# Two transformer blocks in one kernel: the modulation product moved from TensorE to VectorE, and the weight stream put into five shared slots

## The reference

```python
def first_block(x, ...):
    h = rmsnorm(x); dq, dk, dv, sq, sk, sv = split(h @ w_qkv)
    diff_o = rmsnorm(diff_attention(dq, dk, dv, lam, rel_bias))   # 4 heads, two softmaxes each
    sb_o = rmsnorm(stick_breaking_attention(sq, sk, sv))          # 8 heads
    x = x + rmsnorm(concat(diff_o, sb_o) @ w_o)
    u = causal_conv(rmsnorm(x) @ w_up)                            # 1024 -> 5632
    return x + rmsnorm((gelu(gate) * val) @ w_down)               # 2816 -> 1024

def second_block(x, c, ctx, c_ctx, ...):
    sh1, sc1, gt1, sh2, sc2, gt2 = split(silu(c) @ w_mod + b_mod, 6)         # 1024 -> 6144
    csh1, csc1, ... = split(silu(c_ctx) @ w_mod + b_mod, 6)                  # two are used
    h = rmsnorm(x) * (1 + sc1) + sh1;  hc = rmsnorm(ctx) * (1 + csc1) + csh1
    q, k, v, f, g_a, g_f = split(h @ w_in)
    attn = windowed_attention(rope(q), rope(k), v, kc, vc, sink)             # 8 query, 2 key heads
    y = (sigmoid(g_a) * (attn @ w_pa) + sigmoid(g_f) * (fft2(f) @ w_pf)) @ w_out
    x = x + gt1 * rmsnorm(y)
    return x + gt2 * rmsnorm(conv_ffn(rmsnorm(x) * (1 + sc2) + sh2))
```

## Time and profile before

| | |
|---|---|
| median of 3 runs | 1582.09 us (1581.15 to 1590.77) |
| profiled execution | 1582.59 us, span 1580.8 us |
| granted clock of PE, mean | 0.976 |
| PE busy | 1494.2 us (95%), 6756 matmuls |
| PE weight loads | 1165.4 us (74%) |
| DVE busy | 794.4 us (50%) |
| ACT busy | 663.7 us (42%) |
| POOL busy | 98.8 us (6%) |
| DMA | 147.74 MB, mean 93 GB/s |
| chain that ended last | PE 81%, DVE 10%, ACT 5%, issue 3% |

### The profile page before, as it was taken

How to read it: one execution, slowest core, us unless ns; L and a number is a source line. 1 busy time by engine, 2 the same in 40 slices (tenths; PEclk the granted TensorE clock), 3 DMA queues, 4 the chain that set the end, 5 groups by cost and what they waited for, 6 DMA issues and landing times.

```text
span 1580.8 us, 17158 instructions
## 1 busy us (share of the span) xinstructions
PE 1494.2 (95%) x6756; PEld 1165.4 (74%) x6756; DVE 794.4 (50%) x1078; ACT 663.7 (42%) x1034; POOL 98.8 (6%) x63
## 2 busy tenths in 40 slices
PE   7999778789999999999999999999998999999995
PEld 5776545567688888888687777788776888888884
DVE  6225449863876666633645433344535544344334
ACT  5235547653544544322533444444343433333222
...
GB/s 234 126 80 41 40 54 185 160 233 141 54 107 93 90 98 96 157 94 105 42 51 92 53 41 41 54 45 90 143 84 14 134 93 96 104 93 94 98 36 53
DMA packets 41403, 147.74 MB, mean 93 GB/s; under 512 B 4427, under 2 KB 5451, under 8 KB 40940
## 3 DMA queue, kind: packets, MB, share of 16 engines
...
## 4 chain that ended last, share of the span: by engine, by line
PE 81%; DVE 10%; ACT 5%; issue 3%; DMA 0%; SPq 0%; DVEq 0%; ACTq 0%
PE PS L262 24%; PE PS L263 23%; PE PS L264 23%; PE PS L804 2%; PE PS L771 1%; ACT whi L234 1%; DVE X L1385 1%; DVE wlo L242 1%; ACT L L936 1%; DVE Z L1385 1%; PE PS L373 1%; PE PS L790 1%; DVE DW L1382 1%; DVE DW L1385 1%; DVE small L1478 1%
## 5 line engine op out<-in xcount | busy, mean ns | idle before, releaser
L242 DVE TENSOR_TENSOR wlo<-raw,whi 128x1024 fp32r<-128x1024 f32 x229 | 289.1, 1269 | 316.8 <-ACT whi L234 316.5
L262 PE MATMUL PS<-Hhi,whi 128*128 128x512 f32 x1032 | 414.8, 402 | 13.3 <-DVE wlo L242 6.5
L263 PE MATMUL PS<-Hlo,whi 128*128 128x512 f32 x1032 | 404.6, 392 | 0.0
L264 PE MATMUL PS<-Hhi,wlo 128*128 128x512 f32 x1032 | 404.3, 392 | 0.0
L234 ACT ACTIVATE whi<-raw 128x1024 fp32r<-128x1024 f32 x246 | 255.3, 1049 | 94.3 <-PE PS L264 88.8
L262 PEld LDWEIGHTS PS<-Hhi,whi 128*128 128x128 f32 x1032 | 194.9, 189 | 73.0 <-issue 25.2
L264 PEld LDWEIGHTS PS<-Hhi,wlo 128*128 128x128 f32 x1032 | 195.2, 189 | 42.1
L263 PEld LDWEIGHTS PS<-Hlo,whi 128*128 128x128 f32 x1032 | 195.2, 189 | 39.2 <-issue 1.0
L262 PE MATMUL PS<-Dhi,whi 128*128 128x512 f32 x352 | 136.9, 389 | 0.0
L263 PE MATMUL PS<-Dlo,whi 128*128 128x512 f32 x352 | 136.9, 389 | 0.0
L264 PE MATMUL PS<-Dhi,wlo 128*128 128x512 f32 x352 | 136.9, 389 | 0.0
...
## 6 DMA issues: line engine op xcount, KB each, us to landing
raw<-in_w_up SPq DMA_DIRECT2D x88, 512.0 KB, 3.5
raw<-in_w_down SPq DMA_DIRECT2D x44, 512.0 KB, 3.5
raw<-in_w_mod SPq DMA_DIRECT2D x36, 512.0 KB, 3.5
raw<-in_w_g SPq DMA_DIRECT2D x16, 512.0 KB, 3.5
...
raw<-in_w_o SPq DMA_DIRECT2D x8, 512.0 KB, 4.3
raw<-in_w_out SPq DMA_DIRECT2D x8, 512.0 KB, 4.7
X<-in_x SPq DMA_DIRECT2D x4, 512.0 KB, 8.8
```

Of the source, the lines that this page charges most:

```text
L242: e.tensor_tensor(wlo[i % NH], raw[i % NR], whi[i % NH].bitcast(f32), ALU.subtract).then_inc(q["w_lo"], 1)
L262: e.matmul(o, lhs[0], rhs[0], start=first, stop=False)
L263: e.matmul(o, lhs[0], rhs[1], start=False, stop=False)
L264: return e.matmul(o, lhs[1], rhs[0], start=False, stop=last)
```

## The change

It has two parts.

**The stream.** `NS` = 5 slots of 8 KB a partition take the place of the two rings. In a slot, `raw` and `wlo` are the same 4 KB (the low part is written over the loaded chunk), and `whi` is the other half. A load of chunk i waits for `w_done` of chunk i-5, that is for PE; the copy to `whi` waits for the load alone. 20 KB a partition become free; 12 KB of them hold two buffers `wm` for raw w_mod chunks and the accumulator `macc`.

**The modulation of groups 0 to 8.** The 36 chunks leave the stream, `cx` and `POOL_LO` are gone. SP loads them raw (`mod_load`), two at a time. DVE multiplies the two halves of a chunk (128x512) by a per-partition scalar, silu(c) of that partition's row, and adds to `macc` (`mod_part`): four operations a chunk in groups 0 to 3 (two vectors), two in groups 4 to 8; 104 in all. PE then sums `macc` over the partitions with matmuls against ones (`acc_columns`), 8 of one column for groups 0 to 3, 4 for the others, and `mod_add` follows. `mod_part` runs with two operations at the end of each stick-breaking tick (16 ticks), four in each of the eight w_o iterations, and two in 20 of the 37 ticks of the second block's attention. `acc_columns` stands in stick-breaking tick 8, in the first diff tick, behind the fifth w_o product, behind w_o ahead of `post_stat`, and in five steps of the second attention.

```diff
-NR = NH = 5
+NS = 5
-    raw = [at(f"raw{i}", "RAW", 4096 * i, [128, 1024]) for i in range(NR)]
-    whi = [at(f"whi{i}", "HL", 8192 * i, [128, 1024], f32r) for i in range(NH)]
-    wlo = [at(f"wlo{i}", "HL", 8192 * i + 4096, [128, 1024], f32r) for i in range(NH)]
+    raw = [at(f"raw{i}", "W", 8192 * i, [128, 1024]) for i in range(NS)]
+    wlo = [at(f"wlo{i}", "W", 8192 * i, [128, 1024], f32r) for i in range(NS)]
+    whi = [at(f"whi{i}", "W", 8192 * i + 4096, [128, 1024], f32r) for i in range(NS)]
+    wm = [at(f"wm{i}", "P", 4096 * i, [128, 2, 512]) for i in range(2)]
+    macc = at("macc", "P", 8192, [128, 2, 512])
...
-            if i >= NR:
-                e.wait_ge(*lo_event(i - NR))
+            if i >= NS:
+                e.wait_ge(q["w_done"], i - NS + 1)
...
-            if i >= NH:
-                e.wait_ge(q["w_done"], i - NH + 1)
-            e.activation(whi[i % NH], raw[i % NR], ACT.Copy).then_inc(q["w_hi"], 1)
+            e.activation(whi[i % NS], raw[i % NS], ACT.Copy).then_inc(q["w_hi"], 1)
...
+    MOD_TICK = (1, 2, 4, 5, 7, 9, 10, 12, 13, 15, 17, 18, 20, 21, 23, 24, 26, 28, 29, 31)
+    MOD_STEP = {4: 4, 10: 5, 16: 6, 22: 7, 30: 8}
...
+    def mod_load(e, n):
+        if n >= 2:
+            e.wait_ge(q["mod_acc"], MOD_OPS[n - 1])
+        e.dma_start(wm[n % 2], a["w_mod"][n].rearrange("p (j c) -> p j c", j=2)).then_inc(q[f"wm{n % 2}"], 16)
...
+        def acc_columns(g, bank, at):
+            e.wait_ge(q["mod_acc"], MOD_OPS[4 * g + 4])
+            for n in range(4):
+                for v in range(mod_vectors(g)):
+                    last = e.matmul(PS[:, bank, at + 2 * n + v:at + 2 * n + v + 1], macc[:, v, 128 * n:128 * n + 128],
+                                    ones[:, 0:1], start=True, stop=True)
             last.then_inc(q["mcol"], 1)
...
             if tick >= 2:
                 sb_values(tick - 2)
+            if tick == 8:
+                e.wait_ge(q["head_ln"], 1)
+                acc_columns(0, 5, 0)
             if tick:
                 sb_sums(tick - 1)
...
             if tick == 0:
                 sb_values(14)
+                e.wait_ge(q["head_ln"], 3)
+                acc_columns(1, 5, 0)
                 sb_sums(15)
...
-            for n in (2 * tick, 2 * tick + 1):
-                if n == 0:
-                    e.wait_ge(q["cx"], 3)
-                if n < 4 * MOD_STREAMED:
-                    mod_chunk(n)
...
             last.then_inc(q["w_done"], 1)
+            if o == 4:
+                acc_columns(2, 6, 0)
...
         mod_group_part(0, range(0, 2), 5)
-        e.wait_ge(q["mod"], 9)
+        e.wait_ge(q["mod"], MOD_NTH[2])
+        acc_columns(3, 6, 0)
+        e.wait_ge(q["head_ln"], 8)
         post_stat(0, 7)
...
+        def mod_part(count):
+            for _ in range(count):
+                n, i = mods
+                nv = mod_vectors(n // 4)
+                j, v = i // nv, i % nv
+                k = 2 * (n % 4) + j
+                c, x, o = csil[:, 2 * k + v:2 * k + v + 1], wm[n % 2][:, j, :], macc[:, v, :]
+                if i == 0:
+                    e.wait_ge(q[f"wm{n % 2}"], 16 * (n // 2 + 1))
+                if k:
+                    e.wait_ge(q["mod_acc"], MOD_OPS[n] + i - nv + 1)
+                    stt(o, x, c, o, ALU.mult, ALU.add, "mod_acc")
+                else:
...
+                    ts(o, x, c, 1.0, ALU.mult, ALU.mult, "mod_acc")
+                mods[:] = [n, i + 1] if i + 1 < 2 * nv else [n + 1, 0]
...
             if tick:
                 sb_exponents(tick - 1)
                 sb_log_lo(tick)
+            mod_part(2)
...
             split_to(CH["w_o"] + o + AHEAD)
             if o:
                 post_sum(0, o)
+            if o == 4:
+                mod_add(2, 6, 0)
+            mod_part(4)
...
+            if tick in MOD_TICK:
+                mod_part(2)
```

More of the change, by code:

```diff
@@ L212, in source @@
         return a[name][n]
-    POOL_LO = set(range(CH["w_mod"] + 2, CH["w_o"], 2))
-    N_POOL_LO = [len([c for c in POOL_LO if c <= i]) for i in range(NCHUNK)]
-    def lo_event(i):
-        return (q["w_lo_pool"], N_POOL_LO[i]) if i in POOL_LO else (q["w_lo"], i + 1 - N_POOL_LO[i])
     def load_to(e, state, n):
@@ L327, in sync_program @@
         const("sbmask", sbmask, *CCOL["sbmask"])
-        load_to(e, ld, 16)
+        load_to(e, ld, 8)
+        mod_load(e, 0)
+        mod_load(e, 1)
+        load_to(e, ld, 12)
         e.wait_ge(q["brow"], 8)
         e.dma_start(a["scratch"], brow).then_inc(q["l_brow"], 16)
-        load_to(e, ld, CH["w_mod"] + 9)
+        for n in range(2, 10):
+            load_to(e, ld, 20 + n)
+            mod_load(e, n)
+        load_to(e, ld, CH["w_o"] + NS)
         e.wait_ge(q["l_brow"], 16)
-        e.wait_ge(q["w_done"], CH["w_mod"])
+        e.wait_ge(q["w_done"], CH["w_o"])
         win = bass.AP(tensor=a["scratch"].tensor, offset=127, ap=[[4 * 640 - 1, 128], [640, 4], [1, 512]])
         e.dma_start(BW, win).then_inc(q["l_brow"], 16)
-        load_to(e, ld, CH["w_o"] + 9)
         e.wait_ge(q["mix"], 8)
         e.wait_ge(q["d_tr"], 16)
-        e.wait_ge(q["mcol"], 9)
         e.dma_start(X, a["x"]).then_inc(q["l_xback"], 16)
@@ L357, in sync_program @@
         e.dma_start(ropeS, a["rope"][:, 1, :]).then_inc(q["l_rope"], 16)
-        load_to(e, ld, CH["w_out2"] + 9)
+        for n in range(16, 36):
+            if n >= 18:
+                load_to(e, ld, CH["w_f2"] + ((MOD_TICK[n - 18] + 1) * 38 // 34 + 1) // 2 + NS)
+            mod_load(e, n)
+        load_to(e, ld, CH["w_out2"] + NS)
         e.wait_ge(q["w_done"], CH["w_out2"])
@@ L536, in d_values @@
             last.then_inc(q["d_pv"], 1)
-        def mod_chunk(n):
-            g, i = n // 4, n % 4
-            c = CH["w_mod"] + n
-            e.wait_ge(*lo_event(c))
-            if i == 0 and g:
-                e.wait_ge(q["mrow"], g)
-            for j in range(2):
-                k = 2 * i + j
-                w = cx[:, 4 * k:4 * k + 128]
-                hi, lo = whalf(c, j)
-                e.matmul(PS[:, 6, :], w, hi, start=k == 0, stop=False)
-                last = e.matmul(PS[:, 6, :], w, lo, start=False, stop=k == 7)
-            last.then_inc(q["w_done"], 1)
-            if i == 1 and g:
-                columns_7(g - 1)
-        def columns_7(g):
-            e.wait_ge(q["mod"], g) if g else e.wait_ge(q["qk_ev"], 8)
-            if g in (3, 5, 7, 8):
-                e.wait_ge(q["head_ln"], {3: 5, 5: 6, 7: 7, 8: 8}[g])
-            mod_columns(g, 4, 7)
         for tick in range(20):
@@ L896, in tensor_program @@
         e.wait_ge(q["a_ot"], 16)
+        e.wait_ge(q["mod"], MOD_NTH[8])
         for c in range(8):
@@ L1057, in scalar_program @@
                 sb_weights(15)
-                e.wait_ge(q["sb_qk"], 16)
-                e.wait_ge(q["setup_act"], 1)
-                act(cx[:, 32:160], ones, ACT.Copy, "cx", scale=0.0)
-                act(cx4[:, :, 0:2], csil2, ACT.Copy, "cx")
+                split_to(CH["w_o"] + 4)
             if tick == 1:
                 head_out(3, 4, sbr, sbt, "sb_av", 16)
-            for n in (2 * tick, 2 * tick + 1):
-                if n < 4 * MOD_STREAMED:
-                    split_to(min(CH["w_mod"] + n + AHEAD, CH["w_o"] + 4))
-                    if n % 4 == 3:
-                        if n == 3:
-                            e.wait_ge(q["sb_z"], 16)
-                        mod_row(n // 4, 4, 6, "w_done", CH["w_mod"] + n + 1)
             if tick < 16:
@@ L1507, in vector_program @@
                 d_logits(tick)
-            for n in (2 * tick, 2 * tick + 1):
-                if n < 4 * MOD_STREAMED:
-                    split_to(min(CH["w_mod"] + n + AHEAD, CH["w_o"] + 4))
-                    if n % 4 == 1 and n > 4:
-                        mod_add(n // 4 - 1, 7)
             if tick == 1:
@@ L1807, in gpsimd_program @@
             e.tensor_tensor(G_s, G_s, G_abcd[c % 4], ALU.add).then_inc(q["x_acc"], 1)
-        for i in sorted(POOL_LO):
-            e.wait_ge(q["w_hi"], i + 1)
-            e.tensor_tensor(wlo[i % NH], raw[i % NR], whi[i % NH].bitcast(f32),
-                            ALU.subtract).then_inc(q["w_lo_pool"], 1)
         for c in range(1, 8):
```

133 lines of the change are left out of this document (77 added, 56 removed).

## The result

The changed kernel takes 1627.38 us (median of 4, 1622.13 to 1631.23) against 1583.21 of the kernel before: the ratio is 1.0268, 95% interval 1.0223 to 1.0313. It is slower, as forecast, but by 44 us and not by 26; 1627 lies outside the range of 1585 to 1620. The profiled execution took 1627.65 us.

A forecast was written before the change was run, and what follows sets the result against it. PE was taken as the bound outside stick-breaking (a DVE-ACT chain) and diff attention (DVE's queue), except at short joins. Terms from -21.0 to +15.8 summed to +26.2 us on the profiled 1582.59, forecast 1608 against the median; range 1585 to 1620.

The forecast's parts named there:

- 1 diff stage: Diff-attention stage: DVE's queue is the limit; fewer splits and no POOL contention shorten its path, -21.0 us.
- 2 and 3 stick-breaking and join: Stick-breaking: DVE's sum pairs push the chain, plus columns and half clock, +15.8 us; join to the diff stage +1.2.
- 4 norm behind it: After w_o: acc_columns(3), waiting for the last four sums, stands ahead of post_stat, +4.4 us.
- 6 second attention: Second attention, where PE is full: five acc_columns of four instructions add 5.2 us; DVE's 40 sums lie beside it.
- Rival A: The forecast itself: sum pairs sit on the stick-breaking chain and load landings are paid; 1598 to 1619 us, chance 0.52.
- B: DVE takes stick-breaking sums for nothing, both attention stages shrink by PE's lost work; 1567 or 1553 us, chance 0.12.
- D: Sum pairs hidden in the stick-breaking stage, all else as in Rival A: -12 us, 1597 us, chance 0.12.
- C: Landings hidden, since engines catch up behind each late split: -14.1 us, 1595 us, chance 0.15.
- step 2: Stick-breaking: two DVE sums (a pair, 1.35 us) per tick delay the logits in three of four ticks; +15.8 us.
- step 4: w_o: loads queued behind X and mw make the sixth chunk 4.4 us late, columns 2.1, +6.5; norm behind +4.4.
- step 5: Loads following PE: landings paid at start +3.6 us, V stages +2.3, first down's end +0.7, rope +4.0, w_p +3.5.
- Rival E: Clock: the emptier diff stage leaves PE at 1.2 GHz longer, into w_o; +11 us, 1620 us, chance 0.09.

The follow-up runs named there:

- sums_behind_logits: Changed kernel with each stick-breaking tick's pair of sums moved behind the logits, no longer ahead of the next tick's logits: 1613.83 us (1.019).
- stream_only: Kernel before with only the change's shared slots and loads behind w_done; w_mod stays in the stream, on PE and POOL: 1625.11 us (1.0247).
- pool_back: Changed kernel plus 16 unread 128x1024 subtractions on POOL, released when DVE may start a tick's weights: 1649.73 us, median of two executions (1.042).
- before_dve_lo: Kernel before with POOL's 17 splits moved to DVE: 1579.71 us (0.9977).
- six_both_cols: Changed kernel with six slots, stick-breaking sums behind logits, w_o sums before split, group 3 columns after statistic, groups 0 and 1 columns before values product: 1578.75 us.

## Why the prediction was right or wrong

The sum, step by step, against the profile after:

| step | forecast | measured |
|---|---|---|
| 1 diff stage | -21.0 | -22.6 |
| 2 and 3 stick-breaking and join | +17.0 | +24.3 |
| 4 w_o | +6.5 | +11.1 |
| 4 norm behind it | +4.4 | +6.2 |
| 5 start and V stages | +5.9 | +8.5 |
| 5 end of the down stage | +0.7 | 0 |
| 5 rope | +4.0 | +5.4 |
| 5 w_p | +3.5 | +3.4 |
| 6 second attention | +5.2 | +5.8 |
| none: DFT stage | 0 | +2.1 |

**Right.** The sign, and that the pairs sit on the chain and that the landings are paid. Rival A came out in kind, beyond its own range; B falls with PE's wait for Z, which rose to 24.0 us in the stick-breaking stage where it was to vanish, D with sums_behind_logits, and C with stream_only and with the waits for r, G_b and mt. Several signs came as named: the diff cycle is 20.4 us, PE's wait at rope is 4.2 for 4.3, and w_p was sized within 0.1. The diff stage was right within 2 us and in the main for the reason given: contention is real (pool_back), and its removal pays even with the splits kept (before_dve_lo). That up and down cost nothing held: 422.7 us before and after. Not as named were the length of the stick-breaking stage, 144.0 us for 134 to 137, and a wait of 4 us for wlo in w_o, which did not come.

**Wrong, step 2, the largest miss.** "So it does in three of four ticks. In the fourth DVE idles 3.07 before its split [...] and the pair is hidden." Taking all pairs off that place gave 18.0 us, 1.12 for each of 16; a pair lasts 1.33, so about 13.5 pairs' worth was paid, 3 us more than the 14.85 of the sum. DVE's idle time ahead of that split is a wait for a copy that stands on ACT behind its logarithms, and those wait for the logits that the pair delays. So it moves along with the chain: 3.07 us before the change, 3.06 behind a pair. It was no slack. The columns were the second part: 2.1 us each was about the price at full clock (1.84 to 1.92 measured), and behind the waits they run at half clock, 3.54 and 3.55 us in the changed kernel, 3.5 each by six_both_cols. Together that is some 6 of the 7.3 us missed; the rest isn't assigned.

**Wrong, step 4.** The delay of the load behind X and mw was sized well (11.6 us to land, 13.0 taken from before), but the step followed it to the wrong place. "I get the sixth chunk 4.4 us late": the chunk came in time, its split done 7.6 us before PE could use it, and what came late were the sums that stood behind its split in DVE's queue, with the columns that wait for them on PE. I named what is queued on SP behind the late load, not what is queued on DVE behind the late split. The columns at half clock and the chunk behind them (8.0 us between the starts of the sixth and seventh w_o products in place of 5.44) are the rest. The norm's miss of 1.8 us is the half clock behind PE's wait as well: the granted clock is 0.62 in the 1.65 us of the statistic, and from there to the end of the stage 9.7 us pass where 8.1 did.

**Wrong, step 5, in size.** The start was underestimated by 2.6 us, rope by 1.4, and the DFT stage wasn't in the sum. At the start the longer wait is followed by a stretch at half clock:

```profile
41.10:48.80 7.70, 7.66 (x16) 5.30 (x17) 4.29 (x6) 2.27 (x4) 0.00 (x0) 0.50 0.13 54
```

brow's first matmuls of 33x512 take 2.04 us where they took 1.09. The kernel before had half clock there too, but for some 3.4 us, so the longer stretch costs about 2 us, an estimate from these two lengths. I had priced this in stick-breaking alone. The 2.1 of the DFT stage go with the granted clock, 0.91 for 1.00, and appear and vanish between runs that don't differ there; what lowers the clock stays open.

The 3.2 us that the prediction sets beside its 3.5 for a load come from a fit that the Trainium skill (DMA: Bandwidth & Descriptors, Anatomy of one DMA — SWDGE (gpsimd) path) gives for transfers issued by GpSimd. These loads are issued by SP, with a median of 3.4 to 3.5 us to landing, and the sum went by that.

**Rival E** was half right. The diff stage's clock fell to 0.71 and w_o's first chunk took 7.2 us, no more than before (8.2 between the same starts). Idle matmuls brought 1.3 us back in the diff stage and none in the kernel's time.
